# A fused decoder layer: two modulation chunks, the compressed scores and the negated maximum moved

## What is computed

```
mod = silu(c) @ w_ada + b_ada                     # 9 vectors of 2048: shift, scale, gate x 3
x = x + 0.5 * g1 * swiglu(modulate(rms(x), sh1, sc1))          # 2048 -> 5632 -> 2048
h = modulate(rms(x), sh2, sc2) @ w_in
o_mla = 8 heads of softmax(q k / sqrt(192)) v                  # causal
o_nsa = 8 heads, each  g_c * compressed + g_s * selected + g_w * window
x = x + g2 * (concat(o_mla, o_nsa) @ w_out)
x = x + 0.5 * g3 * swiglu(modulate(rms(x), sh3, sc3))
return rms(x)
```

## Time and profile before

| | |
|---|---|
| median of three runs | 2157.22 us (2157.12 to 2162.86) |
| the profiled execution, its own time | 2158.35 us |
| its span, first to last instruction | 2156.6 us |
| TensorE busy | 2072.9 us, 96% |
| VectorE busy | 1338.5 us, 62% |
| ScalarE busy | 902.9 us, 42% |
| chain that ended last | TensorE 89%, VectorE 4%, DMA 3%, issue 3%, ScalarE 1% |
| granted TensorE clock, mean | 0.981 |
| adds of the modulation (L1506) | 420 instructions, 315.1 us, 750 ns each |
| w_lo (L1488) | 657 instructions, 793.2 us, 1220 ns |
| exponentials (L1418) | 48 instructions, 447 ns, 44.1 us of idle time before them, all put down to L1859 |

### The profile page before, as it was taken

One profiled execution on the slowest core, in us unless ns is written; L12 is line 12 of the kernel. 1 busy time (PEld: TensorE's weight loads), 2 busy tenths in 40 slices (PEclk: granted clock), 3 DMA queues, 4 the chain that ended last, 5 costly groups with the idle time before them and its releaser, 6 DMA issues.

```text
span 2156.6 us, 27935 instructions
## 1 busy us (share of the span) xinstructions
PE 2072.9 (96%) x9500; PEld 1635.1 (76%) x9500; DVE 1338.5 (62%) x1775; ACT 902.9 (42%) x1137; POOL 43.0 (2%) x63
## 2 busy tenths in 40 slices
PE   5989999999999999999999899899999999999997
PEld 2568888888877777787778777788888888877775
DVE  1457666777678887894355775577674444444444
ACT  3244443434434333443444444444444444434332
POOL 1000000000000000000013000000000000000000
PEclk7999999999999999999999999999999999999999
DMA  9978888788788888796766415477775666546553
GB/s 354 379 270 279 264 295 281 258 287 282 266 288 314 300 297 297 247 354 219 223 229 207 141 38 184 144 248 270 269 246 176 195 184 185 184 149 223 189 183 125
DMA packets 271084, 513.31 MB, mean 238 GB/s; under 512 B 15193, under 2 KB 29572, under 8 KB 270504
## 3 DMA queue, kind: packets, MB, share of 16 engines
q1 hardware_dynamic: 270120, 508.37, 70.1%
q10 hardware_dynamic: 896, 4.06, 0.5%
HBM read 508.50 MB, written 3.87 MB: 238 GB/s over the span
## 4 chain that ended last, share of the span: by engine, by line
PE 89%; DVE 4%; DMA 3%; issue 3%; ACT 1%; SPq 0%; POOL 0%; DVEq 0%; ACTq 0%; POOLq 0%
PE ps L645 28%; PE ps L646 28%; PE ps L647 28%; DMA ada_half<-in_w_ada_dram 2%; PE ps L729 1%; PE ps L674 1%; PE ps L703 1%; PE ps L891 1%; DVE ada_acc L1506 1%; PE ps L755 0%; PE ps L687 0%; DVE probs L1855 0%; DVE silu_gate L1619 0%; PE ps L799 0%; DVE w_lo L1488 0%
## 5 line engine op out<-in xcount | busy, mean ns | idle before, releaser
L1488 DVE TENSOR_TENSOR w_lo<-raw,w_hi 128x1024 fp32r<-128x1024 f32 (+1 forms) x657 | 793.2, 1220 | 416.5 <-ACT w_hi L1173 412.2
L1173 ACT ACTIVATE w_hi<-raw 128x1024 fp32r<-128x1024 f32 (+1 forms) x657 | 687.3, 1054 | 833.1 <-PE ps L647 581.6
L645 PE MATMUL ps<-w_hi,hT_hi 128*128 128x512 f32 (+1 forms) x1856 | 744.6, 401 | 9.6 <-POOL hT_lo L606 3.4
L646 PE MATMUL ps<-w_lo,hT_hi 128*128 128x512 f32 (+1 forms) x1856 | 733.9, 395 | 0.0
L647 PE MATMUL ps<-w_hi,hT_lo 128*128 128x512 f32 (+1 forms) x1856 | 733.7, 395 | 0.0
L645 PEld LDWEIGHTS ps<-w_hi,hT_hi 128*128 128x128 f32 x1856 | 351.3, 189 | 104.9 <-issue 15.0
L647 PEld LDWEIGHTS ps<-w_hi,hT_lo 128*128 128x128 f32 x1856 | 351.2, 189 | 84.2
L646 PEld LDWEIGHTS ps<-w_lo,hT_hi 128*128 128x128 f32 x1856 | 351.8, 190 | 81.1 <-issue 1.0
L1506 DVE SCALAR_TENSOR_TENSOR ada_acc<-ada_raw,silu_c,ada_acc 128x512 f32<-128x512 f32 x420 | 315.1, 750 | 7.9
L645 PE MATMUL ps<-w_hi,actT_hi 128*128 128x512 f32 x704 | 283.7, 403 | 3.4 <-DVE silu_gate L1619 3.4
L647 PE MATMUL ps<-w_hi,actT_lo 128*128 128x512 f32 x704 | 279.0, 396 | 0.0
(11 more groups left out here) (202 smaller groups left out, 976.4 us busy)
## 6 DMA issues: line engine op xcount, KB each, us to landing
ada_raw<-in_w_ada_dram SPq DMA_DIRECT2D x224, 512.0 KB, 4.7
raw<-in_w_gate_dram SPq DMA_DIRECT2D x176, 512.0 KB, 4.4
raw<-in_w_up_dram SPq DMA_DIRECT2D x176, 512.0 KB, 4.7
raw<-in_w_down_dram SPq DMA_DIRECT2D x176, 512.0 KB, 4.7
raw<-in_w_in_dram SPq DMA_DIRECT2D x72, 512.0 KB, 4.9
ada_half<-in_w_ada_dram SPq DMA_DIRECT2D x16, 2048.0 KB, 16.1
raw<-in_w_out_dram SPq DMA_DIRECT2D x32, 512.0 KB, 4.7
raw<-in_w_uq_dram SPq DMA_DIRECT2D x9, 512.0 KB, 5.3
```

The costliest lines, as they stand in the source:

```text
L645: pe.matmul(bank, lhs_hi, rhs_hi, start=start, stop=False)
L646: pe.matmul(bank, lhs_hi, rhs_lo, start=False, stop=False)
L1173: act.activation(part(U, w_hi, s), part(U, raw, s), ACT.Copy).then_inc(hi_done, 1)
L1488: dve.tensor_tensor(part(U, w_lo, s), part(U, raw, s), part(U, w_hi, s).bitcast(F32), ALU.subtract)\
```

## The change

Two chunks (30 and 31) leave the head passes. SP loads their pieces between `wout` panels of units 1 to 3, VectorE adds them behind the same panels (`late_steps`: three panels of every four, from panel 0 of unit 1 to panel 4 of unit 3), TensorE turns them after panels (2, 3) and (3, 4), VectorE sums them at (2, 6) and (3, 7). The compressed keys lie in 16 columns beside the selected keys in `kT128` and `kT64`, so that `score` makes both with the same instructions, 144 and 272 columns wide instead of 128 and 256; `maxima` copies the compressed scores out of bank 2 (`cmp_taken`), `score` of pass u waits for that copy of pass u - 2, and `turn_q(16)` no longer waits for `cmp_read`. The scaled and negated maximum comes from L1855's instruction itself (scale -SCALE, minimum), so L1859 and its wait go, and `exps` waits for each tile's own maximum.

```diff
+def late_steps(u, j):
+
+    return [(1 + i // 8, i % 8) for i in range(16) if i * 4 // 3 == (u - 1) * 8 + j]
...
 # SP
-            for e in (1, 2):
-                for p in range(8):
-                    load_ada(Unit("late", e), 0, p)
             for j in range(RING, STAGES["wout"][1]):
                 out_rows(Unit("wout", 0), j)
-            for U in units(sp, "wout", 1, STAGES["wout"][0]):
-                load_unit(U, out_rows)
+            for u in range(1, STAGES["wout"][0]):
+                for j in range(STAGES["wout"][1]):
+                    out_rows(Unit("wout", u), j)
+                    for e, p in late_steps(u, j):
+                        load_ada(Unit("late", e), 0, p)
...
 # TensorE, turn_q, score and project_out
                 if e == HEADS:
-                    pe.wait_ge(A["cmp_read"], TT)
                     pe.wait_ge(pool_step, 18 * TT)
...
+                if u >= 2 and u % 2 == 0:
+                    pe.wait_ge(A["cmp_taken"], min(u // 2, HEADS))
...
-                    w = (t + 1) * P
-                    dst = ps[:, 2 + u % 2, t * P:t * P + w]
+                    c0, w = key_columns(u, t)
+                    dst = ps[:, 2 + u % 2, c0 - CMP_COLS if has_cmp(u) else c0:c0 + w]
+                    keys = slice(key_start(kx) - CMP_COLS * has_cmp(u), key_start(kx) + w)
                     pe.matmul(dst, qkT[:, b, t * P:(t + 1) * P],
-                              kT128[:, kx, 0:w] if nsa else qkT[:, b, SEQ:SEQ + w], start=True, stop=False)
+                              kT128[:, keys] if nsa else qkT[:, b, SEQ:SEQ + w], start=True, stop=False)
...
-                if nsa and u % 2 == 0:
-
-                    g = h // HPG
-                    for t in range(TT):
-                        dst = ps[:, 5, t * SEQ + h * 32:t * SEQ + h * 32 + N_CMP]
-                        pe.matmul(dst, qkT[:, b, t * P:(t + 1) * P], kc128[:, g * N_CMP:(g + 1) * N_CMP],
-                                  start=True, stop=False)
-                        mm = pe.matmul(dst, qkT[:, b, SEQ + t * P:SEQ + (t + 1) * P],
-                                       kc64[:, g * N_CMP:(g + 1) * N_CMP], start=False, stop=True)
-                    mm.then_inc(A["cmp_scored"], 1)
...
-                    if U.first == 0 and j == 6:
+                    if (U.first, j) == (2, 3):
                         turn_ada(Unit("late", 1), 0)
-                    if U.first == 1 and j == 1:
+                    if (U.first, j) == (3, 4):
                         turn_ada(Unit("late", 2), 0)
...
 # ScalarE, exps
-                act.wait_ge(A["neg_done"], u + 1)
                 for t in range(TT):
+                    act.wait_ge(A["maxed"], 2 * u + t + 1)
...
-                                   scale=SCALE, accum_out=row_sum[:, u, t:t + 1]).then_inc(A["exped"], 1)
+                                   scale=-1.0, accum_out=row_sum[:, u, t:t + 1]).then_inc(A["exped"], 1)
...
 # VectorE, maxima
-                    dve.tensor_tensor_reduce(probs[:, u % 2, sl], ps[:, 2 + u % 2, sl], bias[:, h, (1 - t) * P:SEQ],
-                                             1.0, -3e38, ALU.add, ALU.max, row_max[:, u, t:t + 1])\
-                       .then_inc(A["maxed"], 1)
-                dve.wait_ge(A["maxed"], 2 * u + 2)
-                dve.tensor_scalar(neg_max[:, u, :], row_max[:, u, :], -SCALE, None, ALU.mult).then_inc(A["neg_done"], 1)
+                    dve.tensor_tensor_reduce(probs[:, u % 2, t * P:t * P + w], ps[:, 2 + u % 2, c0:c0 + w],
+                                             bias[:, h, (1 - t) * P:SEQ], -SCALE, 3e38, ALU.add, ALU.min,
+                                             neg_max[:, u, t:t + 1]).then_inc(A["maxed"], 1)
+                if has_cmp(u):
...
+                    dve.tensor_copy(norm_tmp[:, :, SEQ + 32 * h:SEQ + 32 * h + N_CMP],
+                                    ps[:, 2, 0:TT * (P + CMP_COLS)].rearrange("p (t n) -> p t n", t=TT)[:, :, 0:N_CMP])\
+                       .then_inc(A["cmp_taken"], 1)
...
 # VectorE, the passes and the output projection
-                if 2 <= s < 10:
-                    add_ada(Unit("late", 1), 0, s - 2)
...
-                if 12 <= s < 20:
-                    add_ada(Unit("late", 2), 0, s - 12)
...
-            sum_ada(Unit("late", 1), 0)
+            dve.wait_ge(pool_step, 18 * TT)
...
                     if j == 1:
                         residual(before(U), gate2)
-                    if (u, j) == (1, 4):
+                    for e, p in late_steps(u, j):
+                        add_ada(Unit("late", e), 0, p)
+                    if (u, j) == (2, 6):
+                        sum_ada(Unit("late", 1), 0)
+                    if (u, j) == (3, 7):
                         sum_ada(Unit("late", 2), 0)
```

More of the change, by code:

```diff
@@ L66 @@
 CMP_FIRST = 4
+CMP_COLS = 16
+def late_steps(u, j):
+    return [(1 + i // 8, i % 8) for i in range(16) if i * 4 // 3 == (u - 1) * 8 + j]
 def cmp_after(g):
@@ L131, in count_chunks @@
         for q, a in chunks:
-            if stage in ("start", "dn0", "win") or (stage, u) == ("late", 2):
+            if stage in ("start", "dn0", "win") or (stage == "late" and u > 0):
                 before[q] = (uses[a], last[a], None if last[a] is None else steps[last[a]] + 1)
@@ L1886, in cmp_logits @@
                 then_wait(dve.memset(cmp_p[:, :, 0:SEQ], 0.0))
-                dve.wait_ge(A["cmp_scored"], HEADS)
+                dve.wait_ge(A["cmp_taken"], HEADS)
                 for t in range(TT):
```

60 lines of the change are left out of this document (37 added, 23 removed).

## The result

The kernel after takes 2136.14 us (median of 4 runs, 2133.26 to 2140.95), the kernel before beside it 2159.87 (4 runs, 2157.12 to 2162.86): a ratio of 0.9897, with a 95% interval of 0.9880 to 0.9914. Forecast was 2136.5. The profiled execution took 2136.15 around a span of 2134.2 (forecast 2137.7 and 2135.9).

What follows compares the result with a forecast made beforehand. TensorE bounds except in the head passes, where VectorE or a ScalarE-VectorE ring sets the pace. Terms 3.5 + 1.1 + 5.1 + 6.2 + 3.3 + 0.55 + 0.93 = 20.7 off 2157.2 give 2136.5 us, range 2133.5 to 2142.

Steps and rivals of the forecast that it cites:

- (a): Passes 2 to 9: TensorE bounds once VectorE loses the adds; 22.15 us falls to 18.65, gain 3.5.
- (b): Passes 0 to 2: no separate compressed scores, no chunk piece before pass 2's maxima; gain 1.1 us (bounds 0.4 and 1.8).
- (c): Passes 9 to 13: the ring of ScalarE and VectorE closes in 3.80 us, not 4.36, without adds; gain 5.1.
- (d): Passes 13 to 15: cmp_read no longer waited for before the first latent head; 11.0 us falls to 4.8, gain 6.2.
- (e): Passes 15 to 23: TensorE bounds throughout; 26.87 us falls to 23.55, gain 3.3.
- (f): End of the passes: TensorE's idle 0.96 us for the last exponential shortens by 0.56; gain taken as 0.55.
- (g): Output projection, column unit 0 to 1: TensorE's stand of 0.93 us before the residual product goes; gain 0.93.
- The added work: Moved adds in output projection units 1 to 3 cost nothing; the compressed-score copy takes 0.2 us of VectorE's free time.
- R1: Rival, chance 0.13: the output projection binds on VectorE, late by 4.2 us over up to three boundaries, 2140.7 us.
- R2: Rival, chance 0.08: TensorE's clock falls behind gaps in the ring of passes 9 to 13, 2140 us.
- R3: Rival, chance 0.03: adds in the passes never set the pace; only (f) and (g) are gained, 2155.5 us.
- R4: Rival, chance 0.02: late chunk pieces hold up VectorE's w_lo and SP's queue, slower than before, 2162 us.

Runs made afterwards that it cites:

- move_only: The kernel before with only the adds, loads and transposes of chunks 30 and 31 moved to their new places: 2149.49 us, ratio 0.9958.
- after_again: The kernel after, unaltered, run and traced a second time: 2135.36 us, ratio 0.9879 to before.
- dense: The kernel after with a chunk piece behind every panel of units 1 and 2, instead of three behind every four panels: 2135.51 us, one run.

## Why the prediction was right, point by point

- **(a), 3.5 forecast, 3.95 measured.** TensorE bounds, as said. A pair takes 5.16, not 5.29 (1190.63 to 1195.79), 0.13 less, three and a half times. The extra columns do cost what the sum took, 1.41 for the scores (1190.63 to 1192.04) against 1.31. The mis-sized term is the base: the 5.99 of the earlier trace rows came from a stretch in which VectorE set the pace, and was counted as TensorE's own work throughout. In move_only, where TensorE sets the pace with the old products, the pair is 5.90 (second fence below), which is 0.09 of the 0.13. First TensorE's timeline of after:

```profile
1190.63 0.41 PE L1074 MATMUL ps<-kT,qkT 128*128 128x144 f32 x2
1190.88 0.41 PE L1077 MATMUL ps<-kT,qkT 128*128 128x144 f32 x2
...
1192.04 0.49 PE L1087 MATMUL ps<-ident,probs 128*128 128x128 f32 x3
...
1195.79 0.41 PE L1074 MATMUL ps<-kT,qkT 128*128 128x144 f32 x2
```

```profile
1185.17 0.39 PE L1048 MATMUL ps<-kT,qkT 128*128 128x128 f32 x2
...
1191.07 0.39 PE L1048 MATMUL ps<-kT,qkT 128*128 128x128 f32 x2
```

- **(b), 1.1 forecast, 3.23 measured (2.98 in after_again): wrong.** The price in "The same 0.81 was paid there at 1.2 GHz, so twice" was right (1.57). The step that failed is the next one, "From the end of the scores on both counts I take 1.1": it let only a part of the products and of VectorE's piece through to the stamp, where the products and VectorE's part came through whole (1.57, and 0.57 with the negation), and it took the low clock as given, while that was shorter in every trace without the products (0.81). The measured gain lies outside the bounds of 0.4 to 1.8.
- **(c), 5.1 forecast, 5.09 measured.** The ring has the three links of the forecast: 0.33, 2.34, 1.14. From VectorE's and ScalarE's timelines:

```profile
1202.82 1.23 DVE L1509 TENSOR_TENSOR w_lo<-raw,w_hi 128x1024 fp32r<-128x1024 f32 x1 [1.01 <-ACT w_hi L1194]
1203.96 0.28 DVE L1878 CUSTOM_DVE_ANT_0 probs<-ps,bias_toeplitz 128x128 f32<-128x128 f32 x1
...
1206.63 1.23 DVE L1509 TENSOR_TENSOR w_lo<-raw,w_hi 128x1024 fp32r<-128x1024 f32 x1 [1.02 <-ACT w_hi L1194]
```

```profile
1204.29 0.40 ACT L1439 ACTIVATE probs<-probs,neg_max 128x128 f32<-128x128 f32 x1 [1.50 <-DVE neg_max L1878]
...
1205.55 1.04 ACT L1194 ACTIVATE w_hi<-raw 128x1024 fp32r<-128x1024 f32 x1
```

 The Trainium skill ("ScalarE: Activation LUTs", section "What ACT_TABLE_LOAD costs") gives an activation with a per-partition bias some 280 ns and 0.833 ns an element; for 128 and 256 elements that is an estimate of 0.39 and 0.49, and the exponentials here take 0.40 and 0.49. The exponential of the earlier trace rows, before, takes 0.40 as well. So what the negation saves in the ring is waiting, not ScalarE's work.
- **(d), 6.2 forecast, 6.24 measured.** TensorE has no gap before `turn_q(16)`, and `cmp_logits` stands ahead of pass 15's maxima as forecast, without a wait in front of them (1220.14 has no bracket): VectorE ends the stage, about 0.1 behind the scores. The prediction took the 11.0 as it stood, and did not say that a part of it was the low clock behind the wait.
- **(e), 3.3 forecast, 3.44 measured**; its steps are the 2.97 and 2.75 of before.
- **(f) and (g), 1.48 forecast, 1.4 measured** in "rest", where executions of one kernel differ by 0.1 (after) to 1.4 (before). The two idle times themselves changed as forecast: the 0.93 before the residual is gone, and the 0.96 for the last exponential is 0.41:

```profile
1244.94 0.55 PE L1087 MATMUL ps<-ident,probs 128*128 128x128 f32 x3 [0.41 <-ACT probs L1439]
```

- **The added work.** The copy L1884 is 0.18 (0.2 taken) and lies in VectorE's idle time. R1 did not come (no wait for L1640; VectorE was busy for 20.43 of the 22.49 between two residuals, 91%, where the forecast had 95%), and dense shows where it would begin. R2 did not come: the clock is 1.00 from 1179 through the ring. R3 is refuted by move_only (8.0 us in passes 2 to 23), R4 by the absence of any wait of VectorE for `ada_raw` in units 1 to 3.
- **The range.** Its upper end does not follow from its parts: the bounds of the unknown costs add up to 2.6, R1 is 4.2 and R2 up to 3.5, so that the worst of all together is about 2147, not 2142.

The sum was 1.7 short on the span: (b) 2.1, (a) 0.45, (e) 0.14 and the two last terms -0.1, less 0.95 for the later start. That the median of the runs was hit to 0.4 is partly luck. The forecast started from 2157.2 for before, the median of three, and took 20.7 off; the medians measured side by side, 2159.87 and 2136.14, lie 23.7 apart. The gain was 3.0 short and the starting point 2.7 low, and the two cancel.

## What to carry over

Read each stage's bound from a stamp that every iteration leaves, and price an edit as what is left until the next engine's bound; where two engines lie within 0.1 us of each other, single edits will look small and the sum of them is larger than its parts (15.2 and 18.7 here). A ring over two engines is worth more broken than shortened: shortening it by 0.56 a pass and taking the adds out won 5.1, and making one of its links a step earlier, in every second step, won another 4.2. Work that was moved beside a bound engine was free here as long as the other engine was still idle before the stage's last hand-over, and the profile shows that idle time as a number (0.99 to 1.75). And a wait of the bound engine can cost more than its own length: behind the 1.90 of move_only the clock was low, for another 1.9.
